# Feed-forward weights in quarters: the first quarter sum by a second load and an adding DMA instead of VectorE

## What is computed

```
def swiglu_ffn(x, w_in, w_out):                  # w_in (1024, 2*2816), w_out (2816, 1024)
    gate, up = jnp.split(x @ w_in, 2, axis=-1)
    return (jax.nn.silu(gate) * up) @ w_out

for i in range(2):
    x = x + 0.5 * swiglu_ffn(rmsnorm(x, norm_g[i, 0]), ffn_w_in[i, 0], ffn_w_out[i, 0])
    ...                                           # pooling, or convolution
    x = x + 0.5 * swiglu_ffn(rmsnorm(x, norm_g[i, 2]), ffn_w_in[i, 1], ffn_w_out[i, 1])
```

## Time and profile before

| What | us |
|---|---|
| median of three runs | 2588.95 (2587.72 to 2589.30) |
| the profiled execution, first to last instruction (span) | 2585.3 |
| median less span | 3.65 |
| TensorE busy | 2552.6 |
| VectorE busy | 1904.1 |
| ScalarE busy | 1264.0 |
| POOL busy | 191.5 |

### The profile page before, as it was taken

How to read it: one execution, slowest core, us unless ns; L and a number is a source line. 1 busy time by engine, 2 the same in 40 slices (tenths; PEclk the granted TensorE clock), 3 DMA queues, 4 the chain that set the end, 5 groups by cost and what they waited for, 6 DMA issues and landing times.

```text
span 2585.3 us, 43699 instructions
## 1 busy us (share of the span) xinstructions
PE 2552.6 (99%) x17223; PEld 2171.8 (84%) x17223; DVE 1904.1 (74%) x3109; ACT 1264.0 (49%) x2140; POOL 191.5 (7%) x248
## 2 busy tenths in 40 slices
PE   9999999999999989999999999999999999999999
PEld 7787878887777768999988999989999864889998
DVE  5765655686666678877769777688777698897775
ACT  5544445456665654444454444454444413444444
POOL 1110101013000010000020000010000421100000
PEclk9999999999999999999999999999999999999999
DMA  4222222122222212333322332223323472322232
GB/s 137 84 82 67 82 67 92 40 82 102 81 81 73 73 50 82 107 114 107 99 99 82 115 99 98 99 82 105 108 98 99 127 180 75 98 98 99 98 100 81
DMA packets 171883, 241.78 MB, mean 94 GB/s; under 512 B 6545, under 2 KB 149403, under 8 KB 171443
## 3 DMA queue, kind: packets, MB, share of 16 engines
q1 hardware_dynamic: 164755, 216.27, 25.7%
q0 software_dynamic: 6368, 21.79, 3.0%
q10 hardware_dynamic: 576, 1.16, 0.1%
HBM read 233.54 MB, written 5.58 MB: 92 GB/s over the span
## 4 chain that ended last, share of the span: by engine, by line
PE 88%; DVE 6%; ACT 2%; issue 2%; DMA 1%; POOL 0%; SPq 0%; POOLq 0%; DVEq 0%; ACTq 0%
PE ps L2000 8%; PE ps L2002 8%; PE ps L2001 8%; PE ps L440 5%; PE ps L442 5%; PE ps L441 5%; PE ps L2020 5%; PE ps L2021 5%; PE ps L2022 5%; PE ps L858 5%; PE ps L860 4%; PE ps L859 4%; PE ps L2748 1%; DMA w_raw<-in_ffn_w_out_dram 1%; DVE probs L1814 1%
## 5 line engine op out<-in xcount | busy, mean ns | idle before, releaser
L858 PE MATMUL ps<-h_hi,w_hi 128*128 128x512 f32 x608 | 255.2, 420 | 2.5 <-DVE w_lo L417 1.3
L2020 PE MATMUL ps<-a_hi,w_hi 128*128 128x512 f32 x640 | 250.2, 391 | 4.6 <-DVE a_lo L2315 4.6
L2122 ACT ACTIVATE wg<-w_raw 128x512 fp32r<-128x512 f32 x256 | 153.7, 624 | 197.7 <-PE ps L2002 98.0
L2021 PE MATMUL ps<-a_lo,w_hi 128*128 128x512 f32 x640 | 249.8, 390 | 0.0
L2022 PE MATMUL ps<-a_hi,w_lo 128*128 128x512 f32 x640 | 249.5, 390 | 0.0
L860 PE MATMUL ps<-h_hi,w_lo 128*128 128x512 f32 x608 | 237.9, 391 | 0.0
L859 PE MATMUL ps<-h_lo,w_hi 128*128 128x512 f32 x608 | 237.8, 391 | 0.0
L2000 PE MATMUL ps<-mix_late,wg 128*128 128x256 f32 x832 | 235.2, 283 | 0.1
L2002 PE MATMUL ps<-mix_late,wg 128*128 128x256 f32 x832 | 234.7, 282 | 0.0
L2001 PE MATMUL ps<-mix_late,wg 128*128 128x256 f32 x832 | 234.6, 282 | 0.0
L417 DVE TENSOR_TENSOR w_lo<-w_raw,w_hi 128x2048 fp32r<-128x2048 f32 x90 | 206.1, 2290 | 29.4 <-ACT w_hi L412 29.4
(11 more groups left out here) (463 smaller groups left out, 6614.4 us busy)
## 6 DMA issues: line engine op xcount, KB each, us to landing
w_raw<-in_ffn_w_in_dram SPq DMA_DIRECT2D x88, 1024.0 KB, 5.1
w_raw<-in_ffn_w_out_dram SPq DMA_DIRECT2D x44, 1024.0 KB, 4.9
w_raw<-in_a_w_in_dram SPq DMA_DIRECT2D x24, 1024.0 KB, 5.4
w_raw<-in_b_w_in_dram SPq DMA_DIRECT2D x16, 1024.0 KB, 5.4
w_raw<-in_conv_w_pw_dram SPq DMA_DIRECT2D x12, 1024.0 KB, 5.9
shifted<-glu_scratch POOLq DMA_DIRECT2D x32, 264.0 KB, 7.5
w_raw<-in_a_w_out_dram SPq DMA_DIRECT2D x8, 1024.0 KB, 4.9
w_raw<-in_b_w_out_dram SPq DMA_DIRECT2D x8, 1024.0 KB, 4.9
```

The costliest lines, as they stand in the source:

```text
L858: nc.tensor.matmul(dst, wh[:, w], h_hi[:, k], start=k == 0, stop=False)
L2020: nc.tensor.matmul(dst, wh[:, w], a_hi[:, buf, k], start=h == 0 and k == 0, stop=False, skip_group_check=h == 1)
L2021: nc.tensor.matmul(dst, wh[:, w], a_lo[:, buf, k], start=False, stop=False, skip_group_check=h == 1)
```

## The change

VectorE's first sum is taken out of all places of `dve_steps` and `dve_ff`. In its place:

- After the load of each mixed gate or up tile, SP issues a second load (`sum_load`): corner(1, 0) of the same tile, from HBM again, 128 x 4 x 128 values (256 KB, runs of 512 bytes), straight into `mix_s1`. Ahead of it SP waits until lo 5 and sum 6 of the previous mixed tile are done, and for a statistic's broadcast, since `n_sum` is shared with the sums of squares.
- POOL then issues an adding DMA (`sum_add`): corner(1, 1) of the landed tile, added onto `mix_s1`. Ahead of it POOL waits for the tile and for the second load.
- ScalarE's hi 5 and VectorE's sums 6 and 7 wait for the adding DMA (16 counts) instead of for the VectorE sum.
- `gp_ff` puts the 18 adds of a feed-forward into POOL's order, behind the sums of squares that precede it.

```diff
                 else:
-                    act.wait_ge(mix_sum[x], i + 1)
+                    act.wait_ge(mix_sum[x], 16 * (i + 1) if x == 5 else i + 1)
...
-                if x == 5:
-                    dve.wait_ge(raw_loaded[t % 2], 16 * (t // 2 + 1))
-                    low_before(dve, f, s, u, 5)
-                    ins = tt(mix_s1, corner(t, 1, 0), corner(t, 1, 1), ALU.add)
-                elif x == 6:
-                    dve.wait_ge(mix_sum[5], i + 1)
+                if x == 6:
+                    dve.wait_ge(mix_sum[5], 16 * (i + 1))
                     low_before(dve, f, s, u, 6)
                     if i:
                         dve.wait_ge(mix_sum[3], i)
                     ins = tt(mix_s2, mix_s1, corner(t, 0, 0), ALU.subtract)
                 elif x == 7:
-                    dve.wait_ge(mix_sum[5], i + 1)
+                    dve.wait_ge(mix_sum[5], 16 * (i + 1))
...
+        def sum_load(sp, f, s, u, src):
+
+            i = mixed_before(f, s, u)
+            sp.wait_ge(bcast_ready, SPREAD.index(FF_STAT[f]) + 1)
+            low_before(sp, f, s, u, 5)
+            if i:
+                sp.wait_ge(mix_sum[6], i)
+            sp.dma_start(mix_s1, src.rearrange("p (j k) (i n) -> p j i k n", j=2, n=P)[:, 0, 1]).then_inc(mix_first, 16)
+
+        def sum_add(pool, f, s, u):
+
+            t, i = step_tile(f, s, u), mixed_before(f, s, u)
+            pool.wait_ge(raw_loaded[t % 2], 16 * (t // 2 + 1))
+            pool.wait_ge(mix_first, 16 * (i + 1))
+            pool.dma_start(mix_s1, corner(t, 1, 1), accum_op=ALU.add).then_inc(mix_sum[5], 16)
+
+        def gp_ff(pool, f):
+
+            for s in range(PLAIN, FF_STEPS):
+                for u in "gu":
+                    sum_add(pool, f, s, u)
...
         def dve_steps(dve, f, r):
             a, b = 2 * r + 1, 2 * r + 2
             add_pair(dve, f, r - 1, 5)
-            quarter_sum(dve, f, b, "g", 5)
             quarter_low(dve, f, a, "u", 2)
...
             quarter_low(dve, f, b, "g", 5)
-            quarter_sum(dve, f, b, "u", 5, 7)
+            quarter_sum(dve, f, b, "u", 7)
             quarter_low(dve, f, b, "g", 6, 2)
...
+        FF_STAT = (2, 4, 5, 8)
...
                         load(sp, t + n, src)
+                    if u != "o" and step >= PLAIN:
+                        sum_load(sp, f, step, u, src)
...
             gp_sums(pool, 4)
+            gp_ff(pool, 1)
             gp_sums(pool, 5)
+            gp_ff(pool, 2)
```

More of the change, by code:

```diff
@@ L1901, in build @@
         mix_sum = {x: sem(f"mix_sum{x}") for x in (5, 6, 7, 3)}
+        mix_first = sem("mix_first")
         mix_hi, mix_lo, mix_done = sem("mix_hi"), sem("mix_lo"), sem("mix_done")
@@ L2456, in dve_steps @@
             low_half(dve, f, b, 0)
-            quarter_sum(dve, f, a + 2, "g", 5)
             low_half(dve, f, b, 1)
@@ L2469, in dve_steps @@
             quarter_low(dve, f, a + 2, "g", 3)
-            quarter_sum(dve, f, a + 2, "u", 5)
             quarter_low(dve, f, a + 2, "g", 7, 4)
@@ L2506, in dve_ff @@
             hs_sum(dve, f, 6)
-            quarter_sum(dve, f, 2, "g", 5)
             ff_product(dve, f, 1, 1)
@@ L2522, in dve_ff @@
             quarter_low(dve, f, 2, "g", 3, 7, 4)
-            quarter_sum(dve, f, 2, "u", 5)
             quarter_low(dve, f, 2, "u", 1)
@@ L2550, in dve_ff @@
             low_half(dve, f, 2, 1)
-            quarter_sum(dve, f, 3, "g", 5)
             quarter_low(dve, f, 3, "g", 1, 5)
@@ L2559, in dve_ff @@
             quarter_sum(dve, f, 3, "g", 3)
-            quarter_sum(dve, f, 3, "u", 5, 6)
+            quarter_sum(dve, f, 3, "u", 6)
             quarter_low(dve, f, 3, "g", 3, 7, 4)
@@ L3488, in _ @@
             gp_sums(pool, 2)
+            gp_ff(pool, 0)
             pool.wait_ge(band_stored, 16)
@@ L3500, in _ @@
             gp_sums(pool, 8)
+            gp_ff(pool, 3)
         @block.scalar
```

## The result

The changed kernel takes 2760.38 us (2754.87 to 2762.96), the kernel before on the same chip 2589.12: a ratio of 1.0662 (1.0649 to 1.0675), 171 us slower. The direction was forecast, the size was not: 2663 with a range to 2735.

The account below looks back on a forecast made before the run. TensorE was taken to set the time, VectorE counting only where TensorE waits for it. 48 + 28 - 2.4 = 74 us on 2588.95 gave 2663 us, range 2610 to 2735.

Parts of the forecast that it names:

- What goes (-2.4): VectorE's 72 first sums removed: four TensorE waits behind `a_lo` in step 2 shorten by 2.4 us in all, 4.6 at most.
- The load and the add: Per mixed tile: second load 2.8 us alone (2.4 to 5.1), adding DMA 3.9 us from issue (2.5 to 5.1).
- u8, 48 us for 16 places: Up tiles of even steps 4 to 10: first sum late, TensorE stops 3.0 us at 16 places, 48 us.
- Steps 3 and 4, 28 us: First pair of each feed-forward: TensorE stops 2.4 and 4.7 us, together 7.1, four times: 28 us.
- The other tiles, 0 us: Gate and up tiles of step 7, tiles of step 2: buffer free early or VectorE's queue hides both DMAs, 0 us.
- g8, 0.6 us: Gate tile of step 8: its late sum 6 delays the next up tile's load 0.6 us, making the stop 3.0.
- The clock: Rival: clock falls to half rate after each of 24 stops, 3.4 us each, 82 more, 2745; chance 15%.
- both landing times: Sign of being right: POOL's adds land about 3.9 us after issue, SP's second loads 3 to 4.
- Sum 7's wait: Sign of being right: VectorE idle ahead of sum 7 on even steps' up tiles, 5 to 8 us instead of 2.25.
- the join's stop: Sign of being right: TensorE idle before quarter 5 of the next gate tile, until a join, 16 times about 3 us.
- a clock below 1.00: Sign of being wrong: a granted clock below 1.00 in the feed-forwards.
- stops elsewhere: Sign of being wrong: TensorE's stops at other places than forecast, behind hi or lo values.

Follow-up runs that it names:

- even_up: Changed kernel with load and adding DMA only for the 16 up tiles of even steps 4 to 10, VectorE adding the other 56: 2666.83 us.
- not_odd_gate: Changed kernel with load and adding DMA for all tiles but the 16 gate tiles of odd steps, which VectorE adds: 2692.76 us.
- others: Changed kernel with load and adding DMA only for the 40 tiles in neither `even_up` nor `odd_gate`, VectorE adding the other 32: 2607.71 us.
- odd_gate_held: `odd_gate` with the load of the same step's up tile held back until the gate tile's add has landed: 2591.19 us.
- odd_gate: Changed kernel with load and adding DMA only for the 16 gate tiles of odd steps 3 to 9, VectorE adding the other 56: 2622.67 us.
- no_add: Changed kernel without the adding DMA, the second load alone releasing the readers, so results are not the reference's: 2586.96 us.

## Why the prediction was wrong

**What goes (-2.4): wrong, 0.** VectorE had no gap ahead of lo 4 of u2, but with S1 taken out one opens. The same stretch after:

```profile
1024.90 0.69 DVE L2393 TENSOR_TENSOR wu<-w_raw,wu 128x512 fp32r<-128x512 f32 x1 [0.64 <-ACT wu L2123]
```

VectorE now waits 0.64 us for ScalarE's rounding of quarter 1 of u2, which had been ready just as S1 ended. TensorE's four waits behind `a_lo` stay, 4.8 us for 4.6. The step asked what VectorE does there, not what it would wait for next.

**The load and the add: right for a quiet queue.** 2.8 us alone (the shortest landing was 2.7) and 3.9, as taken. POOL needs 0.53 us (median) from the landing to its issue, where 0.1 was assumed.

**u8, 48 us for 16 places: the chain is right, the size nearly, with a slip in the sum.** `even_up` has 49.2, but that close a fit is partly luck: the 3.0 us count a delay of 0.6 from g8, which `even_up` does not have. `not_odd_gate` has it, and 57.1, 3.6 each. And the sum holds quarter 5 of g4 twice, as one of the 16 places and as the second half of "steps 3 and 4": 12 us too many.

**Steps 3 and 4, 28 us: the total is right by luck.** 17.6 at u3 and 9.2 at g4 are 26.8, where 9.6 and 18.8 were forecast. The step took sum 6 of g3 as on time, at 1050.46; in the changed kernel it starts at 1055.07, for g3 is itself one of the odd gate tiles, the next step below. With g3's sum on VectorE (`others`), the stops at u3 are 13.2.

**The other tiles, 0 us: this step failed.** "The buffer for g7 and for step 2 is free many us ahead" is true and was taken for the end of the question. What the two DMAs then meet was not worked out: two 1024 KB loads issued within a us ahead of the second load, and one beside the add; by `odd_gate_held` the stop comes from the one beside the add. Every DMA of this kernel was priced alone or behind its own tile, and "0 us beyond the queueing counted" covered the rest with a share of 31%. A mean share says little, for the loads come in bursts: in `odd_gate`, while g7's second load waits, the share is 1.02:

```profile
1162.00:1169.00 7.00, 7.00 (x56) 6.74 (x55) 2.99 (x6) 3.00 (x4) 0.00 (x0) 1.00 1.02 333
```

Measured: 24.7 us of stops and 12.4 of clock in `odd_gate`.

**g8, 0.6 us: right for what it assumed.** It took u7's S1 as on time; in `not_odd_gate`, where g7 is on time, lo 4 of u7 is 0.4 us late and the stop 0.4 longer than in `even_up`. With g7 late, u7 and g8 follow, lo 4 of u7 is 2.9 us late, and the even steps' stops grow from 3.2 to 4.8.

**The clock: a rival at 15%, and it came true on top of the forecast.** It was priced at 82 us, 3.4 for each of 24 stops; 56.5 came, with 27 falls where before had 2, some 2.3 for each new one. The 3.4 took TensorE as busy for all 6.8 us at 0.50, where the row has 5.26. Set as a rival beside the forecast, it should have been a term of it: for stops of 3 us the only row at hand spoke for a fall.

So 74 forecast became 172 in the trace: -12 for the double count, +2.4 for the gain that is none, about +30 at the odd steps (22.3 at `pe_half`, 8.0 at quarter 5 of u5 to u9), about +22 at the even gate tiles of steps 6 to 10 (57.6 for 12 x 3.0), -1 at steps 3 and 4, and +56.5 of clock; together 172 within rounding.

Of the signs named beforehand, both landing times came as described (medians 3.9 and 3.5). Sum 7's wait and the join's stop came at the places named and were longer: 8.6 us each for 5 to 8, and 4.2 for about 3. Of the three that were to show the prediction wrong, a clock below 1.00 came (0.96 in each feed-forward), and stops elsewhere, though behind `add_pair` and the joins and not behind hi or lo values.

## What to carry to other kernels

When work leaves an engine for a chain of DMAs, price each DMA among the transfers that run at that moment, not alone and not by the mean share; then ask what stands behind the waiting instruction in its engine's order, since here a new order, with the same DMAs and the same buffer, won back the whole 171 us. Stops that are forecast at some us each belong into the sum with the clock's price, not into a rival. And before an engine is relieved, take its work out with as little as possible in its place: `no_add`, which keeps only the second loads, shows in one run that there was nothing to win.

## What the runs showed of the hardware

An adding DMA of 256 KB within SBUF, 512 B runs, takes 3.9 us from POOL's issue when nothing else runs, the same as a plain 512 KB one; POOL itself is busy 1.28 us. The Trainium skill ("DMA: Bandwidth & Descriptors", Anatomy of one DMA) would have it at an estimate of 2.6.

Beside a 1024 KB load on SP's queue that is issued within 0.6 us of it, the add is not so much slowed as started late. In 12 of the 16 places of `odd_gate` its first packet goes 5.1 us after issue (median; 1.85 in `even_up` and `odd_gate_held`), when 0.69 to 0.91 of the load's packets have gone, and it lands 2.6 us after that, 2.1 in the quiet runs. In the other four, at g3, the load is issued 0.8 to 1.2 us ahead of the add, and the add lands after 5.2 to 6.1. The Trainium skill ("DMA: Bandwidth & Descriptors", Queues, rings and completion order) says that a DMA engine takes packets from its queues in turn; by that the add should have begun beside the load, and these traces do not show that. Why it starts late is open.
